# Two transformer blocks with routed experts: ones from a memset, gathers alone in the queue, and a product with a diagonal

## The reference

```
first block:   h = rms_norm(x);  q, k, v, xr, xg, xc = split(h @ w_in)
               x += concat(attention, gated recurrence, convolution, each normed) @ w_out
               h2 = rms_norm(x)
               x += experts(h2)        # 32 experts in 4 groups, each token goes to 2 of them
second block:  h = rms_norm(x) * (1 + scale) + shift      # scale and shift from w_mod and c
               x += mixer(h @ w_in_2) (Fourier mix beside a gated delta rule, with a context of 256 tokens)
               x += experts(rms_norm(x), modulated)
               out = rms_norm(x)
```

## Time and profile before

| | us |
|---|---|
| median of 3 runs | 1863.8 (1860.18 to 1866.36) |
| profiled execution, its own time | 1857.55 |
| its span | 1855.7 |
| PE busy | 1713.0 (92%) |
| VectorE busy | 644.1 (35%) |
| ScalarE busy | 447.8 (24%) |
| GpSimd busy | 170.1 (9%) |
| mean granted clock of TensorE, share of full | 0.956 |

### The profile page before, as it was taken

The page is one execution under the profiler, slowest core; times in us unless marked ns, Lnnn a source line. Parts: engine busy times, 40 slices in busy tenths (PEclk is TensorE's granted clock), DMA queues, the critical chain, the costliest instruction groups (busy, mean ns, idle before and its releaser), DMA issues.

```text
span 1855.7 us, 21811 instructions
## 1 busy us (share of the span) xinstructions
PE 1713.0 (92%) x8742; PEld 884.5 (48%) x8742; DVE 644.1 (35%) x1196; ACT 447.8 (24%) x787; POOL 170.1 (9%) x172
## 2 busy tenths in 40 slices
PE   6999999879999999999589998999599999999983
PEld 2455565544444555555245547975333333333331
DVE  3279221242113121222249947542522221212213
ACT  2233552213312122111258512331000000000001
POOL 0000000010111111110000023100011111111100
PEclk9999999979999999999889998999699999999996
DMA  9265521389999999999480091034699999999994
GB/s 361 91 223 186 165 109 46 125 279 400 396 396 410 407 404 407 405 410 411 169 305 1 5 141 46 1 152 197 229 383 401 397 411 406 406 418 409 422 410 167
DMA packets 94076, 515.26 MB, mean 278 GB/s; under 512 B 22413, under 2 KB 28141, under 8 KB 69400
## 3 DMA queue, kind: packets, MB, share of 16 engines
q1 hardware_dynamic: 82776, 496.46, 69.1%
q0 software_dynamic: 11200, 17.39, 2.8%
HBM read 506.09 MB, written 27.05 MB: 287 GB/s over the span
## 4 chain that ended last, share of the span: by engine, by line
PE 69%; DMA 14%; issue 8%; DVE 5%; SPq 2%; ACT 2%; POOLq 0%; POOL 0%; DVEq 0%
PE bank L845 21%; PE bank L861 10%; PE bank L451 8%; PE bank L459 8%; DMA ring<-in_w_up 5%; DMA ring<-in_w_down 4%; PE bank L802 3%; PE bank L832 3%; PE bank L723 2%; DMA arena<-in_w_up 2%; PE bank L872 2%; PE bank L678 2%; PE bank L444 2%; PE bank L517 2%; DVE arena L2541 1%
## 5 line engine op out<-in xcount | busy, mean ns | idle before, releaser
L847 PE MATMUL bank<-ring,arena 128*64 128x512 f32 x928 | 417.7, 603 | 0.0
L845 PE MATMUL bank<-ring,arena 128*64 128x512 f32 x752 | 339.7, 605 | 8.4 <-DMA ring<-in_w_up 5.5
L861 PE MATMUL bank<-ring,arena 128*64 128x512 f32 x544 | 249.6, 602 | 2.4 <-DMA ring<-in_w_down 2.4
L863 PE MATMUL bank<-ring,arena 128*64 128x512 f32 x544 | 249.6, 602 | 0.0
L451 PE MATMUL bank<-arena,ring 128*128 128x512 f32 x560 | 244.9, 593 | 0.0
L2440 DVE TENSOR_TENSOR arena<-arena,bank 64x512 f32<-64x512 f32 x70 | 48.3, 690 | 558.2 <-ACT arena L1753 558.2
L845 PEld LDWEIGHTS bank<-ring,arena 128*64 128x64 f32 x752 | 100.8, 139 | 208.3 <-issue 201.9
L845 PE MATMUL bank<-arena 128*64 128x512 f32 x368 | 168.5, 612 | 6.7 <-DMA arena<-in_w_up 6.2
L1420 POOL DMA_INDIRECT arena<-xnd,smalli x70 | 67.6, 966 | 1092.9 <-PE bank L832 533.4
L1753 ACT ACTIVATE arena<-bank 64x512 f32<-64x512 f32 x70 | 41.2, 588 | 521.3 <-PE bank L847 521.3
L451 PEld LDWEIGHTS bank<-arena,ring 128*128 128x128 f32 x560 | 105.4, 191 | 127.4 <-issue 127.3
(11 more groups left out here) (434 smaller groups left out, 2004.9 us busy)
## 6 DMA issues: line engine op xcount, KB each, us to landing
ring<-in_w_down SPq DMA_DIRECT2D x62, 2048.0 KB
ring<-in_w_up SPq DMA_DIRECT2D x54, 2048.0 KB
ring<-in_w_gate SPq DMA_DIRECT2D x45, 2048.0 KB
arena<-in_w_gate SPq DMA_DIRECT2D x19, 2048.0 KB, 23.2
ring<-in_w_mod SPq DMA_DIRECT2D x12, 2048.0 KB
ring<-in_w_in SPq DMA_DIRECT2D x10, 2048.0 KB
arena<-in_w_up SPq DMA_DIRECT2D x10, 2048.0 KB, 28.8
ring<-in_w_out SPq DMA_DIRECT2D x4, 2048.0 KB
```

The source lines that it names most:

```text
L845: pe.matmul(GU[0:CAP, :], x, wg_[:, c, :], start=(c == 0), stop=(c == KD - 1), skip_group_check=True)
L847: mm = pe.matmul(GU[CAP:2 * CAP, :], x, wu_[:, c, :], start=(c == 0), stop=(c == KD - 1), skip_group_check=True)
L861: pe.matmul(Y[0:CAP, :], x, wd_[:, c, 0:512], start=(c == 0), stop=(c == 3), skip_group_check=True)
L863: mm = pe.matmul(Y[CAP:2 * CAP, :], x, wd_[:, c, 512:1024], start=(c == 0), stop=(c == 3), skip_group_check=True)
```

## The change

It has five parts.

- First norm: the ones for the sum of squares are a tile that VectorE fills by a memset, and each product waits for its own pair. The wait for `params` stands behind the product. In every `take_root` the table load is issued ahead of the wait for the bank.
- Gathers: SyncE, after the four writes to `xnd`, waits until the second gather of the stage has landed before it issues anything more.
- Head of the second mixer: ScalarE writes a diagonal matrix with the tile's reciprocal roots. PE multiplies each piece of x with it, which transposes and scales at once; `xn2` is gone. ScalarE empties the first half of each tile from a C bank, VectorE the second half from a V bank.
- `last_states` moves ahead of the sums.
- Last scatters: the last scatter but one goes behind the overflow loop as well, and the loop's own outputs use another tile (`ys_beyond`), so that ScalarE and VectorE don't wait for `stored0` before it.

```diff
@@ tiles
+        ones_now = area(5, 0, P)
+        ys_beyond = xTs[1]
-        xn2 = chunks(area(4, 0, 4096), D)
+        diag_r = chunks(area(4, 0, TT * P), P)
@@ TensorE, first norm
-            pe.wait_ge(S("params"), 16 * 2)
...
-            colsum(C, "ss_x", M["ones"], [sq8[:, k, :] for k in range(0, KD, 2)], "sq_pairs", KD // 2)
+            b = C.deal(pe, "ss_x")
+            pe.wait_ge(S("consts"), 3)
+            for k in range(0, KD, 2):
+                pe.wait_ge(S("sq_pairs"), k // 2 + 1)
+                mm = pe.matmul(b[:, :], ones_now, sq8[:, k, :], start=(k == 0), stop=(k == KD - 2))
+            mm.then_inc(C.full, 1)
+            pe.wait_ge(S("params"), 16 * 2)
@@ TensorE, head of the second mixer
-                pe.wait_ge(S("xn2"), t + 1)
-                for half in range(2):
-                    b = C.deal(pe, f"turnX{t}{half}")
+                pe.wait_ge(S("rms_ready"), TT + t + 1)
+                for half, banks in enumerate((C, V)):
+                    b = banks.deal(pe, f"turnX{t}{half}")
                     for j in range(4):
-                        mm = pe.transpose(hd(b, j), xn2[:, t, P * (4 * half + j):P * (4 * half + j) + P], M["ident"])
-                    mm.then_inc(C.full, 1)
-            pe.wait_ge(C.free, C.at(f"turnX{TT - 1}1"))
+                        k = 4 * half + j
+                        mm = pe.matmul(hd(b, j), x_tok[:, t, P * k:P * k + P], diag_r[:, t, :], start=True, stop=True)
+                    mm.then_inc(banks.full, 1)
+            pe.wait_ge(C.free, C.at(f"turnX{TT - 1}0"))
+            pe.wait_ge(V.free, V.at(f"turnX{TT - 1}1"))
@@ SyncE, experts(m)
                     sp.dma_start(xnd[m][P * t:P * t + P, :], xn_tok[:, t, :]).then_inc(S("xn_out"), 16)
+                sp.wait_ge(S("gathered1"), 16 * (BASE[m] // 2 + 1))
@@ GpSimd, experts(m)
-                for n in range(NB[m] + 3):
+                for n in range(NB[m] + 2):
...
-                                in_=ys[0], in_offset=None, bounds_check=4 * T - 1, oob_is_err=False)\
+                                in_=ys_beyond, in_offset=None, bounds_check=4 * T - 1, oob_is_err=False)\
...
+                scatter(NB[m] - 2)
                 scatter(NB[m] - 1)
@@ ScalarE, take_root
+                act.preload_act_table_set(LN_EXP)
                 b = take(name, banks)
-                act.preload_act_table_set(LN_EXP)
@@ ScalarE, beyond part of experts(m)
-                if m == 0:
-                    act.wait_ge(S("stored0"), 16 * ((n0 + NB[m]) // 2))
...
-                            A(ys[0], Y[:, :], ACT.Copy).then_inc(baton, 1)
+                            A(ys_beyond, Y[:, :], ACT.Copy).then_inc(baton, 1)
@@ ScalarE, head of the second mixer
-                    A(rstd[:, t:t + 1], rstd[:, t:t + 1], ACT.Exp, scale=-0.5).then_inc(S("rms_ready"), 1)
+                    chain(A(rstd[:, t:t + 1], rstd[:, t:t + 1], ACT.Exp, scale=-0.5))
+                    A(diag_r[:, t, :], M["ident"], ACT.Copy, scale=rstd[:, t:t + 1]).then_inc(S("rms_ready"), 1)
                 if t:
-                    for half in range(2):
-                        b = take(f"turnX{t - 1}{half}")
-                        for j in range(4):
+                    b = take(f"turnX{t - 1}0")
+                    for k in range(4):
...
@@ VectorE
+            dve.memset(ones_now, 1.0).then_inc(S("consts"), 1)
...
-                if m:
-                    dve.wait_ge(S("stored0"), 16 * ((n0 + NB[m]) // 2))
...
             experts(0, range(TT))
+            last_states()
...
-                    if t == 0:
-                        last_states()
                 if t:
-                    dve.wait_ge(S("rms_ready"), TT + t)
-                    TS(xn2[:, t - 1, :], x_tok[:, t - 1, :], rstd[:, t - 1:t], None, ALU.mult).then_inc(S("xn2"), 1)
+                    b = take(f"turnX{t - 1}1")
+                    for k in range(4, KD):
+                        ins = TS(hT0[:, k, P * (t - 1):P * t], hd(b, k - 4), aX[:, k:k + 1],
+                                 mc[:, MC.index("x0"), k:k + 1], ALU.mult, ALU.add)
+                    ins.then_inc(V.free, 1)
```

More of the change, by code:

```diff
@@ L1795, in _ @@
                     chain(A(rstd[:, t:t + 1], ssq[:, t:t + 1], ACT.Ln, bias=eps, scale=1.0 / D))
-                    A(rstd[:, t:t + 1], rstd[:, t:t + 1], ACT.Exp, scale=-0.5).then_inc(S("rms_ready"), 1)
+                    chain(A(rstd[:, t:t + 1], rstd[:, t:t + 1], ACT.Exp, scale=-0.5))
+                    A(diag_r[:, t, :], M["ident"], ACT.Copy, scale=rstd[:, t:t + 1]).then_inc(S("rms_ready"), 1)
                 if t:
-                    for half in range(2):
-                        b = take(f"turnX{t - 1}{half}")
-                        for j in range(4):
[L1801 to L1804, removed]
+                    b = take(f"turnX{t - 1}0")
+                    for k in range(4):
+                        ins = A(hT0[:, k, P * (t - 1):P * t], hd(b, k), ACT.Identity, scale=aX[:, k:k + 1],
+                                bias=mc[:, MC.index("x0"), k:k + 1])
+                    ins.then_inc(C.free, 1)
             def root2(n):
@@ L2483, in experts @@
                             dve.wait_ge(S("beyond_y1"), i + 3)
-                            STT(ys[0], Y[:, :], stage_w, m5, ALU.mult, ALU.mult).then_inc(baton, 1)
+                            STT(ys_beyond, Y[:, :], stage_w, m5, ALU.mult, ALU.mult).then_inc(baton, 1)
                             settle(dve, S("beyond_st1"), (i + 1) * 16)
```

## The result

| | before | after |
|---|---|---|
| median of the runs, us | 1864.8 (1860.18 to 1866.36, 4 runs) | 1842.15 (1840.28 to 1844.33, 4 runs) |
| profiled execution, its own time, us | 1857.55 | 1842.49 |
| its span, us | 1855.7 | 1840.7 |
| mean granted clock of TensorE | 0.956 | 0.963 |

The change makes the kernel faster: ratio 0.9905, 95% interval 0.9881 to 0.993. That is a gain of some 18 us. The ratio on record is not the quotient of the two medians above, which is 0.9878 and would be 22.7 us. A later set of runs (e12_after_again) gave 0.9907 (0.9882 to 0.9931), with medians of 1843.7 against 1859.0, which are 15.3 apart. Forecast were 1844.4 and a range of 1838 to 1855.

A forecast was written before the change was run, and what follows sets the result against it. PE was taken to bound the first expert stage and transfers the second, with gaps at gathers and stores. Terms 3.6 + 10.6 + 3.0 + 2.2 = 19.4 off 1863.8 gave a median of 1844.4 us, range 1838 to 1855.

The forecast's parts named there:

- First norm: At the kernel's start: first product with w_in starts at 17.6 instead of 21.27, held by its unit's landing; gain 3.6 us.
- Gathers: Ahead of both expert stages: gathers without SyncE's loads beside them shorten from 8.04 and 8.97; gain 10.6 us (0 to 12.8).
- Head of the second mixer: From the first tile's sum to the gates' product: transposing and scaling by a diagonal gains 3.0 us, between 1.3 and 4.8.
- Last scatters: At the ends of both expert stages: scatters issued sooner after their copies; gains 1.7 and 0.5, together 2.2 us.
- the gather alone: Ahead of the expert stages: a gather with nothing beside it takes 3.2 us, near the stores' rows.
- The room for the held stream: Stage 0: held loads still arrive before block 2 wants them, at 407 or later; without room the price is up to 4.8 us.
- The walk: Second mixer's head, tile by tile at half clock: the gates' product starts at 939.8 instead of 941.13, a gain of 1.3 us.
- Rival 1: Both gathers: VectorE, not the queue, holds them; gains 2.3 and 3.3 in place of 10.6, median 1849.4; chance 0.10.
- Rival 2: Stage 0: the weight stream comes late and PE gives 4.8 us back once, median 1849.2; chance 0.07.
- Rival 4: Second mixer's head: the diagonal product becomes the bound, 16 us per tile, kernel slower, median 1891; chance 0.03.
- Rival 3: Both gathers: each takes its 8 us whatever lies beside it; total gain 8.8, median 1855.0; chance 0.05.
- rule of turns between queues: Gathers: DMA engines alternate between queues packet by packet, so by that alone the gathers' term would be near zero.

The follow-up runs named there:

- e12_after_again: The kernel after, unchanged, timed and profiled again beside three other kernels on one chip: 1843.7 us against 1859.0, ratio 0.9907.
- e5: Kernel after with the first w_in unit loaded ahead of `mats` in the queue: 1838.7 us against 1862.6 for before, ratio 0.9878.
- e1: Kernel before with only the first norm's edits: 1858.1 us against 1862.4, ratio 0.9973.
- e2: Kernel before with only SyncE's wait for the gathers' landing: 1851.45 us against 1862.4, ratio 0.9943.
- e7: Kernel after with the second gather behind the first one's landing and SyncE waiting for the first alone: 1840.8 us against 1862.6 for before, ratio 0.9911.
- e3: Kernel before with only the second mixer's new head, including the moved `last_states`: 1858.25 us against 1862.4, ratio 0.9973.
- e6: Kernel after with VectorE summing tile t before it empties the product of tile t - 2: 1839.65 us against 1862.6 for before, ratio 0.9889.
- e8: Kernel after without the overflow loops on all five engines: 1838.05 us against 1862.6 for before, ratio 0.9884.
- e10: Kernel after with last scatters ahead of GpSimd's overflow loop and PE's loop behind the last store's landing: 1848.8 us against 1859.0 for before, ratio 0.9933.
- e4: Kernel before with only the last two scatters behind the overflow loop and the loop's own buffer: 1862.15 us against 1862.4, ratio 0.9987.

## Why the prediction was right

It was right as a whole: 19.4 off the median were forecast; 22.7 lie between the medians, some 18 by the ratio and 15.0 between the two profiles. Its largest terms hold for the reason given. But part of the agreement is luck. The four terms, measured as below, come to 3.6 + 8.2 + 2.4 - 0.4 = 13.8 in the traces, not 19.4. The 2.65 ahead of the second gather, which no term has, brings them near the 15.0; some 1.4 are lost again in the rest of the code. And the median that was forecast, 1844.4, lies so near the measured 1842.15 because the profiled execution of before lies 7.3 under its median and that of after at its own; the 15.0 of the profiles off the 1863.8 would be 1848.8. The lower end of the range, 1838, does not follow from the terms it names either: 3.6 + 12.8 + 4.8 + 2.2 = 23.4 off 1863.8 is 1840.4. Step by step:

- **First norm, 3.6.** L648 at 17.7 as forecast, 3.56 gained, held by the w_in unit as worked out; e5 shows the cap by lifting it. At the first gather it reads 2.67, the lower clock having run for 25.5 us up to there against 23.1 in before; in e1, the same edit alone, it reads 5.83 there, with 22.3. Term and reason stand; the rest goes with the clock, as far as one execution of each can tell.
- **Gathers, 4.8 + 5.8 = 10.6.** Measured 3.97 and 4.25. The mechanism is right, by e2 and e7: loads beside a gather lengthen it. The term that was mis-sized is the gather alone: 3.2, from the stores' rows, where it takes 3.9 to 4.1. A gather's first packet comes 1.7 to 1.8 after its issue and a store's 1.54, and the store's packets are all started 0.2 to 0.5 later. Even so 3.2 was nearer than the rows allowed: of the two stores, the 3.14 had a fetch of instructions beside it, and a store with nothing beside it takes 2.1 to 2.4. PE's two waits for the gathered rows shrank from 9.3 and 11.2 to 5.4 and 4.9, by 10.2; 2.0 of these belong to the write of `xnd` ahead of the second gather, which goes with the new head and not with the gathers. The room for the held stream in stage 0 was real: its next load went out at 390.28 for 396.13, and PE waited for no unit.
- **Head of the second mixer, 3.0.** Measured 2.4 in after, 1.9 in e3; 1.7 to 5.2 between any profile with the old head and any with the new. The size is right within what the traces tell. The walk named VectorE's wait for the product of tile t before it sums tile t + 2; that wait is the 3.66 of the trace, and e6 shows that it hid another 5.0.
- **Last scatters, 2.2.** This step failed. The scatters come 0.77 after their copies as forecast, but the load of y in the chain is issued 5.13 and 6.73 after the copies, for 4.89 and 6.53 in before: -0.2 in each stage, where +0.5 and +1.7 were forecast. I ended the sum at the scatter's issue and took its duration from a row in which the fetch of PE's code had just passed. The earlier issue puts the store's packets under that fetch (e8, e10).
- **Rival 1, VectorE holds the gathers.** Refuted. In after VectorE works for 2.00 of the 2.24 from the gather's issue on, as much as before (2.31 of 2.57), the first packet comes at 1.81, while VectorE is at work, and the gather takes half the time. The rule of the Trainium skill in "SBUF — State Buffer", SBUF: two separate sides, that a VectorE instruction which takes both ports keeps GpSimd from writing its descriptors, shows in no row of this case; whether any of VectorE's instructions beside these gathers takes both ports, no row tells.
- **Rival 2, the stream late.** Did not occur, in after or in e2. **Rival 4, the diagonal product the bound.** 16 passes of a tile took 3.8 at their slowest, far from 9.
- **Rival 3, a gather takes 8 us anyway, and the Trainium skill's rule of turns between queues.** The 8 us are refuted by e2. With loads in flight the first packets came 4.2 to 5.0 after the issue wherever they were looked at (before, e1, e3, e4, e7), in an empty queue 1.7 to 1.8. Once they have begun, the two queues share the DMA engines: in before, from 381 to 385, the gathers' queue moves 0.52 MB and takes 52% of their time, that of the loads 0.51 MB and 54%, and the loads run on to near 391. So a gather does not stand behind all that SyncE has queued, and in that the traces agree with the rule of the Trainium skill in "DMA: Bandwidth & Descriptors", Queues, rings and completion order, that each DMA engine takes turns between the queues. What the prediction drew from it, a term near zero, does not follow: in before the loads cost the two gathers 2.5 each of later start, and 1.5 and 1.7 of shared DMA engines. Why the start is late no run shows.

## What to carry to other kernels

Let a short indirect gather that the matrix engine waits for go ahead of the bulk loads: here a wait on the loading engine for its landing cost nothing, since the stage had buffers in hand, and was worth 4 us a time. When a store is moved earlier, end the sum at its landing and look at what else uses the DMA engines just then, the engines' own instruction fetches at loops among it. Once a stage's copies are shared between engines, look at what the helper does in its own order: emptying one tile before summing the next cost more here (5.0) than the whole rearrangement had gained (2.4). And before a forecast is called right, add up its terms as they were measured: here the total agreed better than they did.

## What was not expected

- One 16 KB fetch of PE's instructions, 0.9 to 1.6 us on one of 16 DMA engines, makes a 2 us store 3.4 to 4.4.
- Another such fetch goes with a write to `xnd` that lands some 2 us later; it is gone in all ten profiled kernels with the new head, and nobody had put it into a sum.
- An overflow loop all of whose bodies are skipped takes GpSimd 5 us: it still runs its 8 turns, with two tests in each.
- Of two gathers issued together in an empty queue the first takes 3.7 to 4.7, one by itself 3.9 and 4.1: the second costs the first little.
- Some 350 us of unchanged code took 350.9 to 358.3, for the most part by how long the clock was at its lower level.
